# Inverse levels of a chunked RWKV-7 mixer: eight 64x64 quarter products with a 64x64 identity in place of two full 128x128 transposes

## The reference: what is computed

```
def _rwkv7_step(S, inp):
    r_t, w_t, k_t, v_t, kk_t, a_t = inp
    sa = jnp.einsum('bshvk,bshk->bshv', S, -kk_t)
    S = S * w_t[..., None, :] + sa[..., None] * (kk_t * a_t)[..., None, :] + v_t[..., None] * k_t[..., None, :]
    y = jnp.einsum('bshvk,bshk->bshv', S, r_t)
    return S, y
```

## Time and profile before

| | |
|---|---|
| device time, median of 3 runs | 1177.79 us |
| lowest and highest run | 1177.7 and 1181.29 us |
| span of the profiled execution | 1173.6 us |
| the profiled execution's own device time | not given apart from the three runs |
| TensorE matmuls busy | 997.6 us, 85% of the span, 12572 instructions |
| TensorE weight loads busy | 609.4 us, 52%, 12572 instructions |
| VectorE / ScalarE / GpSimd busy | 502.5 / 316.8 / 96.0 us |
| mean granted clock of TensorE | 0.925 of full speed |
| bytes moved by DMA | 224.44 MB |

### The profile page before, as it was taken

The page is one execution under the profiler, slowest core; times in us unless marked ns, Lnnn a source line. Parts: engine busy times, 40 slices in busy tenths (PEclk is TensorE's granted clock), DMA queues, the critical chain, the costliest instruction groups (busy, mean ns, idle before and its releaser), DMA issues. The chain is left out here.

```text
span 1173.6 us, 28618 instructions
## 1 busy us (share of the span) xinstructions
PE 997.6 (85%) x12572; PEld 609.4 (52%) x12572; DVE 502.5 (43%) x1378; ACT 316.8 (27%) x733; POOL 96.0 (8%) x128
## 2 busy tenths in 40 slices
PE   3899998778788999999856999879878999999930
PEld 3866666567675465333315655557766465333310
DVE  0103855352625335433116248655566444433226
ACT  1231116332332032212113411355433032212110
POOL 1200000000100000132110000000010000121110
PEclk9899998997899989999987999899989999999975
DMA  9977726243537536899955323200010654899851
GB/s 350 310 216 260 246 92 244 81 154 138 200 135 194 203 130 228 304 390 372 358 188 155 135 95 89 72 3 4 4 46 10 244 180 176 305 383 379 319 205 54
DMA packets 144568, 224.44 MB, mean 191 GB/s; under 512 B 20700, under 2 KB 98761, under 8 KB 143616
## 3 DMA queue, kind: packets, MB, share of 16 engines
q1 hardware_dynamic: 131712, 185.61, 46.4%
q0 software_dynamic: 10592, 29.64, 6.9%
q10 hardware_dynamic: 2128, 7.21, 1.6%
HBM read 216.73 MB, written 21.14 MB: 203 GB/s over the span
## 5 line engine op out<-in xcount | busy, mean ns | idle before, releaser
L1534 ACT ACTIVATE region<-bank 128x512 f32<-128x512 f32 (+3 forms) x322 | 155.1, 512 | 241.7 <-PE bank L1441 73.8
L1415 PE MATMUL bank<-region 128*32 128x512 f32 x1152 | 171.3, 600 | 9.1 <-issue 6.5
L1415 PEld LDWEIGHTS bank<-region 128*32 128x32 f32 x1152 | 48.4, 111 | 112.2 <-issue 112.2
L1153 PE MATMUL bank<-u,ring 128*128 128x384 f32 x320 | 106.5, 488 | 0.0
L1319 PE MATMUL bank<-ring,u 128*128 128x512 f32 x192 | 89.5, 624 | 8.1 <-DVE u L2285 5.9
L1441 PE MATMUL bank<-ring,region 128*32 128x512 f32 x768 | 87.3, 595 | 1.4 <-ACT region L1534 1.4
L1153 PEld LDWEIGHTS bank<-u,ring 128*128 128x128 f32 x320 | 59.9, 190 | 40.5 <-issue 1.4
L2203 DVE COPY_PREDICATED region<-lev,bank 128x256 f32<-128x256 uint8 x90 | 34.4, 443 | 105.4 <-PE bank L976 105.4
L1601 ACT ACTIVATE region<-bank 128x384 f32<-128x384 f32 x50 | 23.7, 492 | 168.7 <-PE bank L1153 96.7
L1319 PEld LDWEIGHTS bank<-ring,u 128*128 128x128 f32 x192 | 37.7, 199 | 54.9 <-issue 44.9
L2418 DVE TENSOR_TENSOR region<-region,bank 128x256 f32<-128x256 f32 x24 | 10.1, 422 | 124.6 <-ACT region L1846 95.7
(11 more groups left out here) (298 smaller groups left out, 1508.6 us busy)
## 6 DMA issues: line engine op xcount, KB each, us to landing
ring<-in_w_mod SPq DMA_DIRECT2D x48, 1024.0 KB
region<-in_moe_w SPq DMA_DIRECT2D x48, 1024.0 KB
ring<-in_moe_w SPq DMA_DIRECT2D x48, 1024.0 KB
ring<-in_w_in SPq DMA_DIRECT2D x20, 768.0 KB
region<-y_rows SPq DMA_DIRECT2D x6, 1024.0 KB, 7.7
region<-g_rows POOLq DMA_DIRECT2D x4, 1024.0 KB, 6.6
ring<-in_w_in SPq DMA_DIRECT2D x12, 256.0 KB
ring<-in_w_out SPq DMA_DIRECT2D x4, 768.0 KB
```

The lines of the kernel that those rows point to most:

```text
L1153: last = pe.matmul(dst[:, 0:T], w[:, c, tc(m)], u[:, c, :], start=(c == 0), stop=(c == KT - 1))
L1415: last = pe.matmul(bank[p % 2][cols, :], xs[:, p % 2, c, cols], of[(p * P + CTILE * q) // CAP][:, c, :], start=(c == 0), stop=(c == KT - 1))
L1534: return act.activation(dst, src, ACT.Copy)
```

## The change

In the turn, the two transposes of a pair are replaced by eight products, one for each direction d, head e and chunk p: the stationary operand is the 64x64 matrix of `xx_m` on the partitions of chunk p, the moving operand the 64x64 identity `half_ident` on the same partitions. The result is the transposed matrix on the partitions of e, in the bank 2j + p and the columns (2 + d)C. Before, direction chose the bank and chunk the columns; now chunk chooses the bank and direction the columns. The second hunk makes L976 read `ut_m` in the new order. `half_ident` was in the constants already.

```
                         for d in range(2):
-                            last = pe.transpose(bank[2 * j + d][:, tc(1)], xx_m[:, j, 2 * d:2 * d + 2, :].rearrange("p e n -> p (e n)"),
-                                                ident)
+                            for e in range(2):
+                                for p in range(2):
+                                    last = pe.matmul(bank[2 * j + p][rows64(e), (2 + d) * C:(3 + d) * C],
+                                                     xx_m[rows64(p), j, 2 * d + e, :], half_ident[rows64(p), :], start=True, stop=True)
                         last.then_inc(t_mm, 1)
...
                                     last = pe.matmul(bank[2 * j + e][rows64(p), d * C:(d + 1) * C],
-                                                     ut_m[rows64(e), j, 4 * d + 2 + p, :], ut_m[rows64(e), j, 4 * p + d, :],
+                                                     ut_m[rows64(e), j, 4 * p + 2 + d, :], ut_m[rows64(e), j, 4 * p + d, :],
                                                      start=True, stop=True)
```

## The result

| | before | changed |
|---|---|---|
| median of the 4 runs of each | 1177.74 us | 1188.88 us |
| lowest and highest | 1172.78 and 1181.29 | 1188.44 and 1192.14 |
| span of the profiled execution | 1173.6 us | 1186.5 us |
| its own device time | not given apart | 1188.44 us |

The ratio is 1.0124, with a 95% interval of 1.0083 to 1.0166: slower by 11 us in the medians and 12.9 us in the spans, where the prediction had 14.8. The forecast of 1192.5 us, with a range of 1175 to 1207, stands against 1188.88. In a later comparison, again with both kernels on one chip, the ratio was 1.013 (1.0081 to 1.0178).

The account below looks back on a forecast made before the run. TensorE's instruction feed, one block of 256 ahead at 3.8 us, was taken to bound the changed levels: layer 1 +8.7 and layer 0 +6.1 make +14.8 us, a span of 1188.4, 1192.6 against the median; forecast 1192.5, range 1175 to 1207.

Parts of the forecast that it names:

- The feed (parts 1 and 3): TensorE gets 2520 more instructions; fed at 3.8 us per block of 256, layer 1 +8.7 us, layer 0 +6.1.
- The array's own time (part 2): Mixer pair slots on TensorE shrink from 0.76 to 0.48 us; 17 us saved together if the instructions are there.
- rival A: Instruction feed is no limit, stops come from weight loads alone; the 17 us saved in full, 1161 us; chance 0.14.
- Layer 0 (part 3): Layer 0's mixer levels, limited by instruction blocks: +3.1 us in step 0, +1.5 each in steps 1 and 2, +6.1.
- The store of 1.7 us a step (part 3): Each step of mixer levels starts with one instruction block in store, taken to hide 1.7 us.
- What lies around the span: The 4.2 us between the 1173.6 us span and the 1177.79 us median, added to the forecast span.
- The later borders (part 5): All later block borders shift by 2520 instructions; effect 0, with 2 us to either side.
- part 4: L976's index, copies and merge cost nothing; weight loads behind the mixer move with its end, so nothing gives time back.
- B: An instruction block is served in about 3.4 us: 14 us less than forecast, 1178 us, no change; chance 0.09.
- C: Gaps lower the engine's clock, or blocks cost 4.0 us and the store hides nothing: 1201, up to 1208 us; chance 0.15.

Follow-up runs that it names:

- experiment 1: Quarter products in layer 1 alone, transposes kept in layer 0, against the kernel before: 1183.13 us, ratio 1.0064.
- experiment 4: Four products of a 64x128 stationary operand in place of the eight quarter products, 16 instructions a slot, against the kernel before: 1210.26 us, ratio 1.03.
- second pair of profiles: Both kernels, unaltered, profiled once more: the kernel before 1174.82 us, ratio 1.0004; the changed kernel 1188.1 us, 1.013.
- experiment 3: Quarter products in some slots only, against the kernel before: pair 0 (30 of 90) 1169.06 and 1167.31 us; pairs 0 and 1 (60) 1182.31 us.
- 30-slot kernel: Quarter products for pair 0 alone, 30 of 90 slots, against the kernel before, run twice: 1169.06 us, ratio 0.995, and 1167.31 us, 0.9934.

## Why the prediction was right, and where it was off

**The feed (parts 1 and 3): shown.** Stops exactly on a grid of 256 instructions, in any line, without weight loads; a starved block (one that TensorE has to wait for) in 3.74 us in the mean where 3.8 was taken; stops of 0.83 to 1.72 us where 1 to 1.7 were expected; the loss in layer 1 alone repeats in experiment 1; the stops go with the number of instructions through 0, 30, 60 and 90 slots, and are missing in layer 1 where half as many instructions cost more array time (experiment 4). Layer 1 was forecast at +8.7 us and gave +9.0 and, in the second pair of profiles, +10.4 (69.8 for 59.4).

**The array's own time (part 2): the slot right, the 17 us not shown.** Uncut slots took 0.51 and 0.47 us against the 0.48 of the sum. Level length less stops fell by 8.5 us in layer 1, where 10.5 were forecast, and by 1.7 in layer 0 for 6.5 (8.9 and 2.1 in the second pair of profiles). In layer 0 the granted clock differs between the kernels' steps, so its figure is rough. Nor do the 15.6 us of the page's busy time show the 17, since 3.9 of them are the matmuls in front of the router, shown below. The gain exists and was overtaken. It is no term of the forecast's sum, which goes by blocks; it is the price of rival A.

**Layer 0 (part 3): right in kind, mis-sized.** +6.1 forecast, +9.0 and +5.7 measured. The allowance of 1.5 us each for steps 1 and 2 was a guess, and held for neither: in the first pair of profiles they were +0.8 and +4.5.

**The store of 1.7 us a step (part 3): held for 90 slots, not for 30.** 6.4 blocks at 3.75 us are 24.1, less the 22.7 of a mean step: 1.4 in store. With 30 slots in experiment 3 the steps found between about 2 and none. It isn't a constant but depends on where the block borders stand when the levels begin.

**What lies around the span: mis-sized.** The 4.2 us between the span of one execution and the median of others were taken for what lies around a span. In the runs that have both, it is 1.7 to 2.5 us, for the changed kernel's profiled run 1.9. So of the 3.7 us by which the forecast's 1192.6 lies above 1188.88, only 1.9 are the span's (1188.4 for 1186.5), and those are the difference of two larger misses: levels 3.2 us longer than forecast, and 5.1 us less elsewhere. That the total came so near is in part luck.

**The later borders (part 5), and part 4's "nothing gives the time back": the terms that failed.** I put 0, with 2 us to either side, and 5.1 us came back outside the level stretches, 5.0 in the second pair of profiles. Two parts of it are visible. First, three long "issue" stops in the expert stage and behind it, before and then changed:

```profile
524.27 7.07 PE L1415 MATMUL bank<-region 128*32 128x512 f32 x64 [1.69 <-issue]
...
563.73 8.77 PE L1415 MATMUL bank<-region 128*32 128x512 f32 x64 [3.33 <-issue]
...
631.92 5.44 PE L1200 MATMUL bank<-u,ring 128*128 128x128 f32 x32 [2.31 <-issue]
```

```profile
528.58 8.77 PE L1417 MATMUL bank<-region 128*32 128x512 f32 x64 [2.09 <-issue]
...
567.94 7.07 PE L1417 MATMUL bank<-region 128*32 128x512 f32 x64 [1.53 <-issue]
...
634.25 5.44 PE L1202 MATMUL bank<-u,ring 128*128 128x128 f32 x32 [2.25 <-issue]
```

7.3 us became 5.9. Second, the clock in front of the router. These are windows over the same 42 matmuls, before and after:

```profile
432.30:441.60 9.30, 9.30 (x42) 8.99 (x43) 3.09 (x14) 4.16 (x9) 2.66 (x1) 0.50 1.04 363
```

```profile
438.98:445.09 6.11, 5.43 (x42) 5.16 (x43) 2.71 (x12) 4.16 (x9) 2.66 (x1) 0.94 1.04 371
```

3.2 us, at the granted level of 1.2 GHz in one and of 2.4 in the other. Both profiles of the kernel before had it low and both of the changed kernel high, but the two profiles of the 30-slot kernel differ in just this place: the router's matmuls took 1.93 us in one and 3.58 in the other. Whether the edit or the single execution sets that clock isn't settled, and what makes up the rest of the 6.3 us between the mixers isn't known.

**Rivals.** A (no limit) is out by experiment 1. B (3.4 us a block for all) is out by the eleven starved blocks, 3.47 to 4.02 us. Its price came from a misreading: counted through the trace, the window 801.86 to 805.26 of the earlier trace rows holds 256 instructions but lies across a border; the block there ran from 801.55 to 805.25, 3.70 us, without a stop. C (starvation spreads, the clock falls) didn't happen: layer 1's mean clocks stayed at 0.97 to 1.00; its upper end, by its own terms, is 1192.5 + 7 + 10 = 1209.5 and not 1208, just as A's "today's 19.8" comes to 6.4 x 3.3 - 1.7 = 19.4. The Trainium skill, Runtime: NRT & Kernel Launch, "Instruction fetch mechanics", was cited for A. Its block of 256 instructions is what these windows count; that the fetch is mostly hidden holds for the kernel before in layer 1, at 4.1 us a block, and not for the changed one; and room for 2048 instructions isn't what a stream shows that runs dry at every 256th, although TensorE had stood idle for 5.5 us just before layer 1's first step.

**Faster than both.** The 64x128 transposes (0.9942 and 0.9939) and the products for pair 0 alone (0.995 and 0.9934) are each 6 to 8 us under the kernel before, and some 20 us under the changed one. That they are faster is measured twice; that the gain is the turn's isn't shown, since the level stretches account for 1 us or less of it in the first profiles.

## What to carry to other kernels

An edit that replaces few large instructions by many small ones has two prices: the array's time, and the instructions' own delivery. Divide the instructions of a stretch by 256 and compare its time with the 3.5 to 4 us that a block took here; a stretch that already runs at one block per 4 us, as layer 1's levels did, has little to gain from a faster array, and loses if the instructions get many more. In this kernel a float32 product counts four of them (two loads, two matmuls), a transpose two. "issue" gaps that recur at a fixed count of instructions, in whatever line, are the sign.

## What was not expected

- A product with a stationary operand of 64 rows by 128 columns took 0.59 us for four (eight records), the transposes of the same shape 0.27 us for four (four records); eight quarter products 0.23 to 0.28. The first two include a change of tile shape behind them. Two row halves side by side brought the float32 product nothing like what four quarters bring.
- Unedited stretches differed by some microseconds: 436 us and 430 between the mixers before and with the change, but 429 and 436 in two profiles of the 30-slot kernel as well. That the borders of the blocks do it isn't shown. Single level stretches of one kernel differed by up to 1.5 us from profile to profile, and the router's clock by execution.
- Fetches under or just behind weight loads stop TensorE in the kernel before as well, for 1.27 to 2.22 us at seven places in layer 0's mixer and for 3.33 us in the expert stage, where 370 GB/s were moving. These stops weren't attacked here.
